# Sums inside a product, roundings and copies in another order, strided loads at another place of their queue: one edit of a kernel that joins two transformer blocks

## The reference, cut to what matters

```python
h = _rms_norm(x, attn_norm[l])
proj = h @ w_in[l]
(q_a, k_c, v_c, k_s, v_s, k_w, v_w, g_a, c_q, c_kv, k_r) = jnp.split(proj, offsets, axis=-1)
q_a = _rope(_heads(q_a, NSA_HEADS), cos_a, sin_a)
k_cmp = _compress(_rope(_heads(k_c, G), cos_a, sin_a), cmp_pos_k[l], cmp_w1_k[l], cmp_w2_k[l])
v_cmp = _compress(_heads(v_c, G), cmp_pos_v[l], cmp_w1_v[l], cmp_w2_v[l])
o_a = _nsa(q_a, k_cmp, v_cmp, _rope(_heads(k_s, G), cos_a, sin_a), _heads(v_s, G),
           _rope(_heads(k_w, G), cos_a, sin_a), _heads(v_w, G), gates)
o_b = _mla(c_q, c_kv, k_r, mla_q_norm[l], w_q_up[l], mla_kv_norm[l], w_kv_up[l], cos_b, sin_b)
mixed = jnp.concatenate([_rms_norm(o_a, nsa_out_norm[l]), _rms_norm(o_b, mla_out_norm[l])], axis=-1)
x = x + mixed @ w_out[l]
h = _rms_norm(x, mlp_norm[l])
x = x + jnp.square(jax.nn.relu(h @ w_ff1[l])) @ w_ff2[l]
```

## Time and profile before

| what | value |
|---|---|
| median of 3 runs | 1654.24 us (1653.69 to 1656.99) |
| the profiled execution | 1653.12 us |
| its span, first to last instruction | 1651.3 us |
| TensorE busy | 1580.5 us, 96% of the span |
| GpSimd busy | 1197.1 us, 72% |
| ScalarE busy | 913.9 us, 55% |
| VectorE busy | 871.0 us, 53% |
| mean granted TensorE clock | 0.995 |
| read from HBM | 276.25 MB |

### The profile page before, as it was taken

One profiled execution on the slowest core, in us unless ns is written; L12 is line 12 of the kernel. 1 busy time (PEld: TensorE's weight loads), 2 busy tenths in 40 slices (PEclk: granted clock), 3 DMA queues, 4 the chain that ended last, 5 costly groups with the idle time before them and its releaser, 6 DMA issues.

```text
span 1651.3 us, 35141 instructions
## 1 busy us (share of the span) xinstructions
PE 1580.5 (96%) x14340; PEld 1515.4 (92%) x14340; DVE 871.0 (53%) x1790; ACT 913.9 (55%) x1549; POOL 1197.1 (72%) x500
## 2 busy tenths in 40 slices
PE   7998999999999999999999999898999998899997
PEld 7986989999999999999999999677999996789997
DVE  6987445993366667777511134956220079552101
ACT  6776665445444445555566656465553356656533
POOL 5653777998887787787888887215888861268885
PEclk9999999999999999999999999999999999999999
DMA  7442555566555555555666656513566664146663
GB/s 248 140 141 65 192 179 169 190 197 189 189 177 172 177 180 169 177 178 171 198 195 196 194 181 178 179 39 128 180 196 196 194 180 141 52 144 195 197 193 115
DMA packets 89631, 279.57 MB, mean 169 GB/s; under 512 B 19200, under 2 KB 19968, under 8 KB 89216
## 3 DMA queue, kind: packets, MB, share of 16 engines
q1 hardware_dynamic: 89472, 277.34, 53.5%
HBM read 276.25 MB, written 1.05 MB: 168 GB/s over the span
## 4 chain that ended last, share of the span: by engine, by line
PE 79%; DVE 8%; ACT 4%; issue 4%; POOL 3%; DMA 0%; DVEq 0%; SPq 0%; POOLq 0%; ACTq 0%
PE ps L2747 21%; PE ps L2091 12%; PE ps L2419 10%; PE ps L2730 7%; PE ps L2731 7%; PE ps L2735 7%; PE ps L538 6%; POOL wl L199 2%; ACT wh L184 1%; DVE attention L1880 1%; PE ps L2716 1%; PE ps L2217 1%; PE ps L2718 1%; ACT attention L1662 1%; DVE small L1885 1%
## 5 line engine op out<-in xcount | busy, mean ns | idle before, releaser
L199 POOL TENSOR_TENSOR wl<-slots,wh 128x1024 fp32r<-128x1024 f32 x236 | 573.0, 2432 | 315.2 <-ACT wh L184 304.1
L2528 POOL TENSOR_TENSOR wl<-slots,wh 128x1024 fp32r<-128x1024 f32 x256 | 619.2, 2422 | 123.9 <-ACT wh L2466 121.8
L2466 ACT ACTIVATE wh<-slots 128x1024 fp32r<-128x1024 f32 x256 | 271.8, 1062 | 345.2 <-issue 219.5
L184 ACT ACTIVATE wh<-slots 128x1024 fp32r<-128x1024 f32 x236 | 249.9, 1061 | 239.0 <-PE ps L2419 98.9
L2730 PE MATMUL ps<-xh,wh 128*128 128x256 f32 x1024 | 242.1, 279 | 0.0
L2747 PE MATMUL ps<-xh,wh 128*128 128x256 f32 x1016 | 239.8, 279 | 1.2 <-ACT wh L2466 1.2
L2731 PE MATMUL ps<-xl,wh 128*128 128x256 f32 x1024 | 239.0, 277 | 0.0
L2747 PE MATMUL ps<-xl,wh 128*128 128x256 f32 x1016 | 237.1, 277 | 0.0
L2730 PEld LDWEIGHTS ps<-xh,wh 128*128 128x128 f32 x1024 | 192.4, 188 | 0.1
L2731 PEld LDWEIGHTS ps<-xl,wh 128*128 128x128 f32 x1024 | 192.5, 188 | 0.0
L2747 PEld LDWEIGHTS ps<-xh,wh 128*128 128x128 f32 x1016 | 190.9, 188 | 1.4 <-ACT wh L2466 1.4
(11 more groups left out here) (385 smaller groups left out, 2994.6 us busy)
## 6 DMA issues: line engine op xcount, KB each, us to landing
slots<-w SPq DMA_DIRECT2D x254, 512.0 KB, 4.1
slots<-wu SPq DMA_DIRECT2D x128, 512.0 KB, 3.6
slots<-wv SPq DMA_DIRECT2D x128, 512.0 KB, 4.1
arena<-bias SPq DMA_DIRECT2D x1, 2048.0 KB, 8.4
attention<-w SPq DMA_DIRECT2D x6, 256.0 KB, 4.7
h<-xT SPq DMA_DIRECT2D x4, 256.0 KB, 6.5
arena<-keys SPq DMA_DIRECT2D x1, 1024.0 KB, 8.7
yT<-y_out SPq DMA_DIRECT2D x2, 512.0 KB, 2.7
```

The source lines that it names most:

```text
L184: act.activation(self.hi[:, n % 2, :], self.slots[:, u % SLOTS, :], ACT.Copy).then_inc(self.rounded, 1)
L199: pool.tensor_tensor(self.lo[:, n % 2, :], self.slots[:, self.order[n] % SLOTS, :], self.hi[:, n % 2, :].bitcast(F32), ALU.subtract).then_ ...
L2466: act.activation(whv[:, r % 2, :], slots_v[:, r % SLOTS, :], ACT.Copy).then_inc(w_hi, 1)
L2528: pool.tensor_tensor(wlv[:, r % 2, :], slots_v[:, r % SLOTS, :], whv[:, r % 2, :].bitcast(F32), ALU.subtract).then_inc(w_lo, 1)
```

## The change

In the order of the code:

- The banks of k2 and v2 change places: v2 is in the one that ur used, k2 in the one of hT.
- SyncE issues the eleven strided loads behind the 18th load of the layer (the second half of V's weights) instead of behind the sixth.
- `parts_of` takes a function that it runs ahead of the seventh chunk; in the feed-forward it is one rounding, which stood behind the eighth.
- ScalarE takes the two latent roots ahead of the copy of q0 and of one rounding, copies cv ahead of the rounding of V's second half, does the tanh of ck between the fifth and the sixth exponential of its group, and three of the last eight exponentials ahead of the copies of ur and uq1.
- In the feed-forward the rounding of the third pair's first unit stands ahead of the root instead of behind it.
- VectorE makes `tile_sum` at the end of `turn_tables` instead of in layer 0, clears Z, X and KR while it waits for the latent roots, and does the silu of ck inside `row_max`, ahead of its maximum.
- TensorE does the sums of the latent squares between the two units of q0 instead of behind them.

No instruction is added or left out.

```diff
@@ -1486,3 +1486,3 @@
             banks.plan([("ck", l), ("uk", l, 0), ("uk", l, 1), ("cks", l), ("uq", l, 0), ("ur", l), ("hT", l),
-                        ("uq", l, 1), ("k2", l), ("v2", l)], mid3)
+                        ("uq", l, 1), ("v2", l), ("k2", l)], mid3)
             for b, n in ((1, ("sc", l)), (0, ("uv", l, 0)), (2, ("uv", l, 1)), (3, ("rq", l))):
@@ -1553,8 +1553,7 @@
 
-                for n, u in enumerate((8, 9, 10, 11, 0, 1, 6, 7, 4, 5, 2, 3, 20, 21, 22, 23)):
+                for u in (8, 9, 10, 11, 0, 1, 6, 7, 4, 5, 2, 3, 20, 21, 22, 23):
                     ring.load(sp, w2[l, u, :, :])
-                    if n == 5:
-                        latent_weights(l)
                 for half in range(2):
                     pair_half(24, half)
+                latent_weights(l)
                 for u in (16, 17, 18, 19, 15):
@@ -1582,5 +1581,7 @@
         def layers_act(act):
-            def parts_of(stage, gain):
+            def parts_of(stage, gain, between=None):
 
                 for c in range(DC):
+                    if c == 6 and between:
+                        between()
                     if c % 2 == 0:
@@ -1638,6 +1639,6 @@
                 ring.round(act, 1)
-                copy(("q", l, 0), raw_q[:, 0:2, :])
-                ring.round(act, 1)
                 take_root(("msn", l), 256, root[:, 0:T])
                 banks.give(take_root(("msn", l), 128, root[:, T:2 * T], slice(T, 2 * T)), ("msn", l))
+                copy(("q", l, 0), raw_q[:, 0:2, :])
+                ring.round(act, 1)
                 b = banks.take(act, ("turn", l)).rearrange("p (k n) -> p k n", n=P)
@@ -1653,4 +1654,5 @@
                 copy(("q", l, 1), raw_q[:, 2:4, :])
-                ring.round(act, 2)
+                ring.round(act, 1)
                 copy(("cv", l), hidden_rows[:, 1, :])
+                ring.round(act, 1)
 
@@ -1687,4 +1689,5 @@
                 exponentials(0, SELECTED, 1, range(4, 8))
-                exponentials(1, WINDOW, 0)
+                exponentials(1, WINDOW, 0, range(5))
                 compressed(("cks", l), 0)
+                exponentials(1, WINDOW, 0, range(5, 8))
                 copy(("uq", l, 0), qN[:, 0:2, :])
@@ -1694,5 +1697,6 @@
                            ("hT", l))
+                exponentials(1, WINDOW, 1, range(3))
                 copy(("ur", l), qRr)
                 copy(("uq", l, 1), qN[:, 2:4, :])
-                exponentials(1, WINDOW, 1)
+                exponentials(1, WINDOW, 1, range(3, 8))
                 for t in range(TT):
@@ -1739,4 +1743,3 @@
                 stage = 2 * l + 1
-                parts_of(stage, p2(l, "mlp"))
-                ring.round(act, 1)
+                parts_of(stage, p2(l, "mlp"), lambda: ring.round(act, 1))
                 squares(stage)
@@ -1744,3 +1747,3 @@
                 keep_h(lambda b: ("wm", l, b))
-                ring.round(act, 1)
+                ring.round(act, 2)
                 banks.give(take_root(("mf", l), D, std[:, 0:T]), ("mf", l))
@@ -1756,3 +1759,4 @@
                 for i in range(1, 16):
-                    ring.round(act, 1)
+                    if i > 1:
+                        ring.round(act, 1)
                     if i == 3:
@@ -1793,2 +1797,6 @@
             ins.then_inc(l_quads, 1)
+            dve.tensor_reduce(tile_sum, const("ident").rearrange("p (j i) -> p i j", i=32), AX.X,
+                              ALU.add).then_inc(l_tiles, 1)
+            dve.wait_ge(l_tiles, 1)
+            dve.tensor_scalar(tile_sum, tile_sum, 0.5, None, ALU.mult).then_inc(l_tiles, 1)
 
@@ -1833,2 +1841,5 @@
                 link(dve.tensor_tensor(sinr[:, 0, :], lconst("sinA"), rst[:, 0:T], ALU.mult))
+                dve.memset(Z[64:128, :, :, T - 1:T], 0.0)
+                dve.memset(X[:, :, :, 30:32], 0.0)
+                link(dve.memset(KR, 0.0))
                 banks.wait_drained(dve, ("msn", l))
@@ -1863,3 +1874,2 @@
                     dve.wait_ge(l_quads, 1)
-                link(dve.memset(KR, 0.0))
                 rope(("rk", l), ckr[:, 1:2, :], cos_b, sin_b, spread_keys)
@@ -1870,3 +1880,3 @@
 
-                def row_max(group, t):
+                def row_max(group, t, between=None):
                     heads = slice(8 * group, 8 * group + 8)
@@ -1882,2 +1892,4 @@
                                    ("s", l, t, c))
+                    if between:
+                        between()
                     for c in range(4 * group, 4 * group + 4):
@@ -1931,9 +1943,2 @@
 
-                dve.memset(Z[64:128, :, :, T - 1:T], 0.0)
-                dve.memset(X[:, :, :, 30:32], 0.0)
-                if l == 0:
-                    dve.tensor_reduce(tile_sum, const("ident").rearrange("p (j i) -> p i j", i=32), AX.X,
-                                      ALU.add).then_inc(l_tiles, 1)
-                    dve.wait_ge(l_tiles, 1)
-                    dve.tensor_scalar(tile_sum, tile_sum, 0.5, None, ALU.mult).then_inc(l_tiles, 1)
                 rope(("rp", l, 0), raw_q[:, 0:2, :], cos_r, sinr, add_to(qA[:, 0:2, :]))
@@ -1958,4 +1963,3 @@
                     projected_keys(i)
-                row_max(WINDOW, 1)
-                silu(("cks", l), 0, 2)
+                row_max(WINDOW, 1, lambda: silu(("cks", l), 0, 2))
                 probabilities(0, SELECTED, 1)
@@ -2081,3 +2085,3 @@
 
-            def split_pair(job, stage=None):
+            def split_pair(job, stage=None, between=None):
 
@@ -2099,2 +2103,4 @@
                     for j in range(2):
+                        if j and between:
+                            between()
                         w = by_chunk(ring.high(pe))
@@ -2228,5 +2234,8 @@
                 split_pair(("ckr", l))
-                split_pair(("q", l, 0))
-                sums(("msn", l), range(2), sqc, ready=(l_sqc, 2 * l + 1), last=False)
-                sums(("msn", l), (2,), sqc, slice(T, 2 * T), ready=(l_sqc, 2 * l + 2), start=False)
+
+                def latent_sums():
+                    sums(("msn", l), range(2), sqc, ready=(l_sqc, 2 * l + 1), last=False)
+                    sums(("msn", l), (2,), sqc, slice(T, 2 * T), ready=(l_sqc, 2 * l + 2), start=False)
+
+                split_pair(("q", l, 0), between=latent_sums)
                 bank = banks.open(pe, ("turn", l))
```

More of the change, by code:

```diff
@@ L1638, in layers_act @@
                 ring.round(act, 1)
+                take_root(("msn", l), 256, root[:, 0:T])
+                banks.give(take_root(("msn", l), 128, root[:, T:2 * T], slice(T, 2 * T)), ("msn", l))
                 copy(("q", l, 0), raw_q[:, 0:2, :])
                 ring.round(act, 1)
-                take_root(("msn", l), 256, root[:, 0:T])
-                banks.give(take_root(("msn", l), 128, root[:, T:2 * T], slice(T, 2 * T)), ("msn", l))
                 b = banks.take(act, ("turn", l)).rearrange("p (k n) -> p k n", n=P)
```

## The result

The changed kernel took **1647.26 us** (median of 5 runs, 1646.81 to 1648.08), the kernel before beside it 1654.56 us (5 runs, 1653.69 to 1656.99). The ratio is 0.9948, its 95% interval 0.9936 to 0.9960: faster by 0.5%. The forecast was 1648.6.

A forecast was written before the change was run, and what follows sets the result against it. TensorE, the busiest engine, was taken as the bound, so only its idle or slow time could be won. Attention -2.8, feed-forward -3.4 and tables +0.6 gave -5.6 us: 1647.5 from 1653.1, 1648.6 as a median; range 1645.8 to 1651.8.

The forecast's parts named there:

- the reduction of 0.39 us and the multiplication: End of the tables: tile_sum's two operations there add 0.39 + 0.18 = 0.6 us, bounds 0 and 2.1.
- rival (b): Tables: the multiplication waits for GpSimd, 1.5 us more, giving 1650.1 us; chance 8%.
- So 1.0 in layer 0: Head of layer 0: earlier latent norms bring the rope ahead of the scores 1.0 us forward; 0 in layer 1.
- Not all of that 1.0 lasts ... I keep 0.4: Behind layer 0's scores: exponentials stay behind V's second-half rounding, so 0.4 of 1.0 us lasts; 1.0 if its load lands earlier.
- I take 1.2 us for each layer: Attention, silu of ck ahead of the row maximum with exponentials and banks moved: 1.2 us per layer, bounds 0.9 and 1.7.
- So 1.07 is what lasts: Silu of ck: of TensorE's 1.7 us wait, only VectorE's 1.07 us idle time at the k2 copy is won.
- I take 0: Strided loads moved behind the layer's 18th load: no gain or loss, 0 us.
- just in time or up to 0.6 us late: Last quarter of ck, loaded behind the strided loads: lands at about 1061 to 1062, at most 0.6 us late.
- VectorE's full list: Attention: VectorE, busy 16.35 of 16.9 us from 1056.3 to 1073.2, is later than ck and covers its lateness.
- Rival (c): Strided loads delay V's second half and its rounding, about 4 us later in each layer: 1657 us; chance 5%.
- So 1.9 us vanish in each layer ... Net 1.7.: Feed-forward start: waits of 1.60 and 0.31 us vanish, the last two parts come 0.2 later; net 1.7 us per layer.
- Rival (a): Only the feed-forward edits count, VectorE's list keeps the attention where it is: 1651.4 us as a median; chance 14%.

The follow-up runs named there:

- experiment 9: The changed kernel once more without a new edit, beside other kernels on one chip: 1644.04 us, 0.9937 of the kernel before.
- experiment 7: Kernel before with only the latent norms' sums inside the first query product and roots ahead of q's copy: 1664.00 us, one execution; kernel before 1668.30 on that chip.
- experiment 12: Kernel before with only tile_sum moved to the end of the tables: 1654.28 us, 1.0001 of the kernel before.
- experiment 2: Changed kernel with the eleven strided loads back behind the layer's sixth load: 1645.14 us, 0.9938 of the kernel before.
- experiment 3: Changed kernel with the silu of ck behind the row maximum again: 1649.01 us, 0.9963 of the kernel before.
- experiment 8: Changed kernel with the copy of cv behind the rounding of V's second half again: 1649.12 us, one execution.
- experiment 1: Kernel before with the feed-forward edits alone: 1649.56 us, 0.9966 of the kernel before.
- experiment 4: Changed kernel with strided loads between the second and third ck loads and tile_sum in VectorE's idle time in layer 0: 1645.70 us, 0.9948 of the kernel before.
- experiment 6: Changed kernel with strided loads in four groups behind the cv loads and tile_sum in VectorE's idle time: 1649.84 us, 0.9901 of the kernel before.

## Why the prediction held, and where it didn't

The forecast was the likeliest case, and the time fell 1.3 us below it, inside the range. That it came so near is in part luck: in experiment 9 the same kernel was 10.6 us below the kernel before, where it was 7.3 here, and the trace beside the prediction's own gives 6.3 against the 5.6 of its sum. Step by step:

- **"the reduction of 0.39 us and the multiplication", 0.6 us of loss.** Right: 0.39 and 0.18 us at 957, ScalarE idle 5.22 instead of 4.70 us, 0.5 us later. The multiplication took 0.18 to 0.20 us in all six traces that have it there, so rival (b) is out.
- **"So 1.0 in layer 0".** The size was right (0.92), the cause was not. I gave it to the earlier norms and let tile_sum's 2.2 us go along in half a sentence. Experiments 7 and 12 each have one of the two and each has the full 0.92: either empties VectorE's list enough, and then TensorE's rotations set the rope. So with the earlier norms in place tile_sum need not have gone to the tables, and the 0.5 us there buys nothing.
- **"Not all of that 1.0 lasts ... I keep 0.4".** This step failed. I took the load that landed at 1051.05 as a bound. It had landed 6.96 us after its issue. In the changed kernel it took 5.71, and so came out as the case that the prediction priced at 1.0. In experiment 7 the same load landed 4.65 us after its issue, its rounding stood at 1054.55, and the exponentials behind it waited 1.18 us for VectorE. In the changed kernel ScalarE was also free before VectorE's maximum. All 0.92 lasted in experiments 2, 7 and 12, 0.8 in the changed kernel, where ck's last quarter took the rest.
- **"I take 1.2 us for each layer" at the silu.** 1.6 in layer 0 and 1.7 in layer 1. "So 1.07 is what lasts" was near: 1.3 for the silu, and VectorE's wait for k2, 1.07 us in both layers before, is 0.12 us in layer 0 and 0.46 in layer 1. The 0.36 us of the other edits I had put inside the wait. The rows of the changed kernel, the silu ahead of the reduction, the new wait for the copy, and k2:

```profile
1069.24 0.40 DVE L1929 SCALAR_TENSOR_TENSOR attention<-attention,ps 30x256 f32<-30x256 f32 x1
1069.57 2.27 DVE L1897 TENSOR_REDUCE small<-attention 128x8 f32<-128x2048 f32 x1
...
1071.35 0.92 PE L2315 MATMUL ps<-attention 128*128 128x256 f32 x3 [0.33 <-ACT attention L1607]
...
1074.59 0.18 DVE L1968 COPY layer<-ps 64x30 f32<-64x30 f32 x1
```

- **"I take 0" for the strided loads.** This step failed in layer 1. I had computed ck's last quarter "just in time or up to 0.6 us late" and covered it with "VectorE's full list". In layer 0 it held. In layer 1 the loads for ck went out a little earlier against their product (the first 6.84 us ahead of it, in layer 0 6.27), but took 5.64 to 7.95 us to land instead of 4.00 to 6.30, and TensorE waited 0.32 and 0.60 us for two quarters, start to start 1.3. Why they landed more slowly there isn't shown; in the traces of experiments 3, 8 and 9 too the last of them took longer in layer 1 (6.7 to 7.8 us) than in layer 0 (6.5 to 6.6). The cover was gone too, because the earlier silu had taken TensorE's next wait for VectorE away: with that wait (experiment 3) 0.3 of 0.9 us lasted. Rival (c) named the right queue, but V was issued first and its second half landed as before (1050.92 in layer 0, 1051.02 before); ck paid. V's first half took 4.73 us instead of 4.00 in layer 0, and the wait of 0.7 us for it was taken back at the rope steps.
- **"So 1.9 us vanish in each layer ... Net 1.7."** The mechanism was right, the term too small: 2.4 vanished, less about 0.1 in layer 0, because rows of waiting leave out 0.35 and 0.17 us of the pipelined ends. Experiment 1 has it without any other edit.

The misses to the good (0.5 and 0.4 in the attention of layer 0, 0.5 at the silu of layer 1, 0.6 and 0.7 in the feed-forward) outweighed those to the bad (1.4 for ck, and 0.8 in unchanged code). Rival (a), the feed-forward alone, would have given 1649.6 by experiment 1; the attention and the tables together gave the rest.

## What to carry to other kernels

Cost a wait of a pipelined engine from start to start, not by its row of idle time: here 1.60 was 1.95 and 0.31 was 0.48. Before a transfer is moved, ask which wait stands behind the one it can miss, and whether another edit of the same change takes that cover away. And a landing in one trace is a sample: look at the same load in the other layer before it bounds anything.

## What the runs showed of the hardware

**Two paces of TensorE at the same granted clock.** The feed-forward loop of layer 0, in the trace before and in that of experiment 7, code and clock (1.00) being the same:

```profile
1165.00:1225.00 60.00, 60.00 (x532) 60.00 (x531) 15.98 (x25) 37.42 (x49) 53.01 (x23) 1.00 0.62 195
```

```profile
1165.00:1225.00 60.00, 60.00 (x512) 60.00 (x511) 14.34 (x23) 35.71 (x46) 51.06 (x22) 1.00 0.59 191
```

532 matmuls against 512 in 60 us, one each 0.113 or 0.117 us, with GpSimd and ScalarE idle longer in the slower one. A pace holds for tens of microseconds and then may change, at other places in each of the 14 traces. Behind the tables, for example, a chunk took 2.83 us instead of 2.72 in four traces, 1.5 us in all: three of the six with tile_sum in the tables and one of the eight without. That is too few to say whether the longer stop brings it on; the cause stays open.

**Half clock behind a stop.** Stretches of 3.4 us at half the granted clock came at other places in each execution. Behind the silu's wait of 1.6 to 1.7 us they came in 4 of 10 cases (5 traces with that wait, two layers each) and cost 1.5 to 1.7 us each. In the 9 traces without that wait none came there. So a part of what the silu edit brings is this chance, which no sum over rows of one trace shows.

**A small copy that takes 0.17 or 2.41 us.** In experiment 9 the last of VectorE's 32x32 copies for the tables was short:

```profile
951.96 0.29 DVE L1793 COPY layer<-layer 32x256 f32<-32x256 f32 x1
952.17 0.17 DVE L1794 COPY layer<-layer 32x32 f32<-32x32 f32 x1
```

In the first trace of the same kernel it was long:

```profile
952.87 0.28 DVE L1793 COPY layer<-layer 32x256 f32<-32x256 f32 x1
953.08 2.41 DVE L1794 COPY layer<-layer 32x32 f32<-32x32 f32 x1
```

Layer 0 began 2.2 us earlier for it than in the other traces with tile_sum in the tables that kept the quick pace. In the trace the short copy starts 0.017 us behind a subtraction of GpSimd (which then took 2.45 us instead of 2.40), the long one 0.025 us behind it; in the twelve other traces the copy was long too, 0.020 to 0.032 us behind. The Trainium skill (SBUF — State Buffer, Who interferes with whom) says of a VectorE instruction in a two-port mode and GpSimd that who issues first gets the shared ports and the other is blocked for the whole instruction. The long copy agrees: it ended with the subtraction. The short one is also recorded behind the subtraction and was not held, so the recorded starts don't show who came first; what decided it stays open.

**One small DMA that holds its queue.** SyncE issued most of the small strided DMAs in 0.47 us each, but in the old and in the changed place the first of them held it longer: 1.91 and 2.17 us in the kernel before, 2.87 and 3.16 behind the loads of V in the changed kernel, 3.25 and 4.15 with two more large loads queued (experiment 4). In experiment 6, four at a time and in layer 0, none took over 0.47 us.
